# A two-block transformer with a product-key expert layer on one core: when weight halves are split, how a bias row is added, and when later weights are loaded

## What is computed

```python
for layer, mixer in ((0, nsa_mixer), (1, moba_mixer)):
    shift, scale, gate = split(silu(c) @ ada_w[layer] + ada_b[layer], 3)
    h = rms_norm(x, norm_g[layer]) * (1 + scale) + shift
    x = x + gate * mixer(h)                 # h @ w_in, attention, (o * silu(z)) @ w_out
shift1, scale1, gate1, shift2, scale2, gate2 = split(silu(c_2) @ w_ada + b_ada, 6)
h = rms_norm(x, norm1_g) * (1 + scale1) + shift1
x = x + gate1 * (concat(norm(o_a), norm(o_b)) @ w_out)   # windowed and 2-D neighbourhood attention
h2 = rms_norm(x, norm2_g) * (1 + scale2) + shift2
x = x + gate2 * peer(h2)                    # 16384 experts, 16 of them per head and token
out = rms_norm(x, final_g)
```

## Time and profile before

| what | value |
|---|---|
| median of 3 runs | 1426.58 us |
| the profiled execution | 1428.41 us, its span 1427.1 us |
| PE busy in the span | 1328.8 us (93%) |
| DVE busy | 1063.2 us (75%) |
| ACT busy | 588.9 us |
| POOL busy | 293.0 us |
| granted clock of PE over the span | 0.967 |

### The profile page before, as it was taken

One profiled execution on the slowest core, in us unless ns is written; L12 is line 12 of the kernel. 1 busy time (PEld: TensorE's weight loads), 2 busy tenths in 40 slices (PEclk: granted clock), 3 DMA queues, 4 the chain that ended last, 5 costly groups with the idle time before them and its releaser, 6 DMA issues.

```text
span 1427.1 us, 22339 instructions
## 1 busy us (share of the span) xinstructions
PE 1328.8 (93%) x8387; PEld 1136.2 (80%) x8387; DVE 1063.2 (75%) x2290; ACT 588.9 (41%) x1099; POOL 293.0 (21%) x205
## 2 busy tenths in 40 slices
PE   5899798988799789999999999999999999999997
PEld 5577665676378556999999999999998888888886
DVE  5687796676577666699977888888977676766676
ACT  0444483354413261545555444444443333333332
POOL 0443102340203003568993000000000000000000
PEclk9899899998899889999999999999999999999999
DMA  9767622575359712424544444444455555555552
GB/s 355 264 217 251 239 68 89 197 271 174 96 176 358 269 53 96 170 88 164 188 151 156 146 147 147 148 147 149 148 196 189 191 190 183 187 191 190 184 187 104
DMA packets 101185, 253.72 MB, mean 178 GB/s; under 512 B 9432, under 2 KB 16856, under 8 KB 100704
## 3 DMA queue, kind: packets, MB, share of 16 engines
q1 hardware_dynamic: 68672, 192.76, 39.6%
q10 hardware_dynamic: 32416, 59.66, 11.7%
HBM read 251.34 MB, written 1.05 MB: 177 GB/s over the span
## 4 chain that ended last, share of the span: by engine, by line
PE 71%; DVE 11%; issue 6%; DMA 5%; POOL 4%; ACT 3%; SPq 1%; POOLq 0%; DVEq 0%; ACTq 0%
PE bank L1679 25%; PE bank L1671 21%; PE bank L698 7%; PE bank L1950 4%; DMA arena<-in_w_ada 3%; PE bank L1112 3%; DVE arena L433 3%; DMA arena<-in_ada_w 2%; PE bank L724 2%; POOL u_lo L1711 2%; PE bank L933 1%; PE bank L806 1%; PE bank L1024 1%; POOL v_lo L1711 1%; DVE arena L975 1%
## 5 line engine op out<-in xcount | busy, mean ns | idle before, releaser
L1671 PE MATMUL bank<-h_hi,u_hi 128*128 128x256 f32 x632 | 182.8, 289 | 4.2 <-POOL u_lo L1711 2.9
L1671 PE MATMUL bank<-h_hi,u_lo 128*128 128x256 f32 x632 | 178.7, 283 | 0.0
L1671 PE MATMUL bank<-h_lo,u_hi 128*128 128x256 f32 x632 | 178.7, 283 | 0.0
L433 DVE SCALAR_TENSOR_TENSOR arena<-arena,silu_c 128x512 f32<-128x512 f32 x140 | 119.9, 856 | 29.4 <-DMA arena<-in_w_ada 15.1
L2133 POOL TENSOR_SCALAR stat<-stat 128x1 f32<-128x1 f32 x2 | 0.4, 190 | 657.0 <-ACT arena L2130 657.0
L1671 PEld LDWEIGHTS bank<-h_hi,u_hi 128*128 128x128 f32 x632 | 121.0, 191 | 5.0 <-issue 2.0
L1671 PEld LDWEIGHTS bank<-h_lo,u_hi 128*128 128x128 f32 x632 | 121.1, 192 | 0.0
L1671 PEld LDWEIGHTS bank<-h_hi,u_lo 128*128 128x128 f32 x632 | 120.9, 191 | 0.0
L1671 PE MATMUL bank<-h_hi,v_hi 128*128 128x256 f32 x392 | 112.9, 288 | 0.8 <-POOL v_lo L1711 0.8
L2046 ACT ACTIVATE u_hi<-raw 128x1024 fp32r<-128x1024 f32 x64 | 67.9, 1062 | 109.2 <-PE bank L1679 109.2
L2046 ACT ACTIVATE v_hi<-raw 128x1024 fp32r<-128x1024 f32 x64 | 67.9, 1062 | 106.0 <-PE bank L1679 106.0
(11 more groups left out here) (277 smaller groups left out, 3557.5 us busy)
## 6 DMA issues: line engine op xcount, KB each, us to landing
raw<-in_u SPq DMA_DIRECT2D x128, 512.0 KB, 3.5
raw<-in_v SPq DMA_DIRECT2D x128, 512.0 KB, 4.2
arena<-in_w_ada SPq DMA_DIRECT2D x96, 256.0 KB, 3.1
arena<-in_ada_w SPq DMA_DIRECT2D x64, 256.0 KB, 3.6
arena<-in_ada_w SPq DMA_DIRECT2D x12, 512.0 KB, 12.0
raw<-in_nsa_w_in ACTq DMA_DIRECT2D x3, 2048.0 KB, 9.4
arena<-in_moba_w_in ACTq DMA_DIRECT2D x3, 2048.0 KB, 12.7
arena<-in_w_in ACTq DMA_DIRECT2D x3, 2048.0 KB, 11.2
```

What stands on the lines that cost most here:

```text
L433: m = V.did(ve.scalar_tensor_tensor(out=acc, in0=src, scalar=factor, in1=acc, op0=ALU.mult, op1=ALU.add))
L1671: last = pe.matmul(zbank[k].t[:, 0:S], u[:, c, :], h[:, c, :], start=n == 0, stop=n == 3 * DC - 1)
```

## The change

- `project_split` calls `ahead.step()` after each quarter's last matmul of the second token half, instead of `ahead.step(4)` after all of them and after `run_later()`. `project_cols_split` steps before `run_later()` too.
- `normalised` (L615) uses `scalar_tensor_tensor` with the identity as both inputs instead of `tensor_scalar`.
- The bias matmul L452 goes. `gate_bias` is zero but for partition 0, where SP loads the bias row of the next gate piece; the first step of a gate piece is then chunk times scalar plus `gate_bias`, and the sum over partitions brings the bias in.
- Sums come due after 13.0 in place of 8.0, transposes after 10.5 in place of 8.5.
- Two tile loads of each mixer move from the z (or v) projections to the start of the attention.
- `trickle(1)` in place of `trickle(2)` in the first z projection; one `trickle(1)` more in each `gated_out`; `gated_out` begins with bank 0.

```diff
         for c in range(DC):
...
-            if c == 0:
+            if c:
+                V.need(m)
+                m = V.did(ve.scalar_tensor_tensor(out=acc, in0=src, scalar=factor, in1=acc, op0=ALU.mult, op1=ALU.add))
+            elif j % 6 < 4:
                 V.need(m_silu, acc_read[k])
                 m = V.did(ve.tensor_scalar(acc, src, factor, None, ALU.mult))
             else:
-                V.need(m)
-                m = V.did(ve.scalar_tensor_tensor(out=acc, in0=src, scalar=factor, in1=acc, op0=ALU.mult, op1=ALU.add))
+                V.need(m_silu, acc_read[k], bias_mark[0])
+                m = V.did(ve.scalar_tensor_tensor(out=acc, in0=src, scalar=factor, in1=gate_bias, op0=ALU.mult, op1=ALU.add))
+                load_bias(m)
...
-                T.need(b.free, m, m_ones, m_bias)
-                pe.matmul(b.t[:], ones[:], acc, start=True, stop=False)
-                acc_read[k] = bias_read[side] = T.did(pe.matmul(b.t[:], ones_row, bias_row, start=False, stop=True))
+                T.need(b.free, m, m_ones)
+                acc_read[k] = T.did(pe.matmul(b.t[:], ones[:], acc, start=True, stop=True))
...
-        acc_read[k] = soon(sum_partitions, 8.0)
+        acc_read[k] = soon(sum_partitions, 13.0)
...
+    def load_bias(free):
+
+        if gate_order:
+            layer, j = gate_order.pop(0)
+            src = a["ada_b"][layer:layer + 1] if layer < 2 else a["b_ada_2"]
+            Y.need(free)
+            bias_mark[0] = ld_bias.did(sy.dma_start(gate_bias[0:1, :], src[:, j * WT:(j + 1) * WT]))
...
-            m_diag[t] = V.did(ve.tensor_scalar(diagonal[t], ident[:], stat[:, t:t + 1], None, ALU.mult))
+            m_diag[t] = V.did(ve.scalar_tensor_tensor(out=diagonal[t], in0=ident[:], scalar=stat[:, t:t + 1], in1=ident[:],
+                                                      op0=ALU.mult, op1=ALU.mult))
...
                 if t == NT - 1 and c % 2 == 1:
                     split_read[s] = m = T.did(last)
+                    if ahead:
+                        ahead.step()
...
             run_later()
-            if ahead and t == NT - 1:
-                ahead.step(4)
...
-    TURN_LAG = 8.5
+    TURN_LAG = 10.5
...
         halves = [range(DC)] if rstd is None else [range(DC // 2), range(DC // 2, DC)]
+
+        turn["proj"] = 0
...
                 load_all(loads)
+                trickle(1)
...
-        project_cols_split(z0, z_cols(zT, 0), z1, (out0, out1))
-        project_cols_split(z1, z_cols(zT, 1), None, (moba_kv,))
+        project_cols_split(z0, z_cols(zT, 0), z1, (out0,), 1)
+        project_cols_split(z1, z_cols(zT, 1))
         run_later(True)
+        load_all((out1, moba_kv))
...
-        project_cols_split(moba_z0, z_cols(zT, 0), moba_z1, (moba_out1,))
-        project_cols_split(moba_z1, z_cols(zT, 1), None, (qa,))
+        project_cols_split(moba_z0, z_cols(zT, 0), moba_z1)
+        project_cols_split(moba_z1, z_cols(zT, 1))
         run_later(True)
+        load_all((moba_out1, qa))
...
-        project_cols_split(kb, kb_use, vb_tile, (mix_out1,))
+        project_cols_split(kb, kb_use, vb_tile)
...
-        project_split(vb_tile, v_use(vb), None, (query0,))
+        project_split(vb_tile, v_use(vb))
         m_vb = V.last()
         run_later(True)
+        load_all((mix_out1, query0))
```

More of the change, by code:

```diff
@@ L411, in ada_steps @@
         acc = ada_acc[k]
-        if j % 6 >= 4:
-            side = j % 2
-            settle(bias_read, side)
-            bsrc = a["ada_b"][layer:layer + 1] if layer < 2 else a["b_ada_2"]
-            Y.need(bias_read[side])
-            bias_row, ones_row = gate_bias[32 * side:32 * side + 1, :], ones[32 * side:32 * side + 1, :]
-            m_bias = ld_bias[side].did(sy.dma_start(bias_row, bsrc[:, j * WT:(j + 1) * WT]))
         for c in range(DC):
@@ L455, in sum_partitions @@
             ada_mark[layer, j] = b.free
-            pe_us[0] += 0.9 if j % 6 < 4 else 2.0
-        acc_read[k] = soon(sum_partitions, 8.0)
-        if j % 6 >= 4:
-            bias_read[j % 2] = acc_read[k]
+            pe_us[0] += 0.9
+        acc_read[k] = soon(sum_partitions, 13.0)
     def gate_of(layer, j):
@@ L466, in build @@
     gate_bias = carve([P, WT], layers)
-    ld_bias = [Load(nc, st, f"ld_bias{i}") for i in range(2)]
-    bias_read, gate_read = [None, None], [None, None]
+    ld_bias, bias_mark, gate_read = Load(nc, st, "ld_bias"), [None], [None, None]
+    gate_order = [(0, 4), (0, 5), (1, 4), (1, 5), (2, 4), (2, 5), (2, 10), (2, 11)]
+    def load_bias(free):
[4 more added lines that the diff above has]
+            bias_mark[0] = ld_bias.did(sy.dma_start(gate_bias[0:1, :], src[:, j * WT:(j + 1) * WT]))
     fillers = [(0, j) for j in range(6)] + [(1, j) for j in range(4)] + [(2, j) for j in range(4)] + [(1, 4), (1, 5)] + \
@@ L512, in first_sums @@
         m = T.did(last)
-        if which == 0:
-            bias_read[:] = [m, m]
-        else:
+        if which:
             acc_read[:] = [m, m]
@@ L772, in project_cols, with project_cols_split @@
                 load_all(loads)
-    def project_cols_split(tile, use, ahead=None, loads=()):
+    def project_cols_split(tile, use, ahead=None, loads=(), steps=2):
         if ahead and tile.n < 4:
@@ L785, in project_cols_split @@
             pe_us[0] += 2.9
-            run_later()
             if ahead:
                 ahead.step()
+            run_later()
             b.free = use(i, b.t[:, 0:S], m)
-            trickle(2)
+            trickle(steps)
             if i == 0:
@@ L1214, in build @@
         finish()
+        G.need(m_a)
+        m_zero = G.did(po.memset(gate_bias[:], 0.0))
         for tile in (kv0, q0, cmp0):
             tile.load(Y)
+        load_bias(m_zero)
         ask_chunks()
```

## The result

The changed kernel takes **1414.65 us** (median of 4 runs, 1413.32 to 1415.94) against 1426.23 for the kernel before (median of 4). The ratio is 0.9914, 95% interval 0.9896 to 0.9933, so it is 12.3 us faster, by the interval 10 to 15. I had said 1390 us and a range down from 1411: the direction was right, two thirds of the gain are missing, and the time lies outside the range. The profiled execution spans 1411.9 us, against 1427.1 in that of before.

A forecast was written before the change was run, and what follows sets the result against it. PE was the engine to watch in the first 568 us, with DVE making it late. The terms summed to 36.6 us off 1428.4, giving 1391.8, and 1.8 lower as a median: 1390 us, range 1374 to 1411.

The forecast's parts named there:

- Third mixer: Third mixer's projections: 4 MB of loads move out and PE's 4.1 us sum wait shrinks; 5.0 us won, between 0 and 6.
- rival A: DVE stays late on chunk waits, losing terms of first z projection, second mixer's start and third mixer; 1408 us, chance 0.22.
- Quarters split early: Projections: ACT's splits ahead of a copy shorten three PE waits for lo halves; 6.0 us won, plus 3.6 of clock.
- Bias matmul: Gate pieces: dropping the bias matmul saves PE 1.0 us at four of eight places; 4.0 us won.
- Transposes later: PE's wait for POOL before a transpose goes, as it now stands behind 8 more matmuls; 2.7 us won.
- Loads moved: Two loads issued as each attention begins share DMA engines with chunks; 1 us lost each, -3.0 in all.
- First mixer's z projection: Fewer filler steps and later loads bring the second compressed-score chain earlier; 6.5 us won, less 4.0 for DVE not following.
- End of the second attention: Only one gate sum is forced, so the output product starts near 373.5 instead of 380.73; 7.3 us, plus 1.5 of clock.
- The diagonal: Norms: the two-input form of L615 is blocked by POOL's split as well; 0 us won.
- rival B: The two-input diagonal escapes POOL's block and falls to about 0.3 us in three places; 1384 us, chance 0.10.
- Rival C: ACT's early splits wait for the tile's DMA, so 6.0 + 3.6 us are lost; 1400 us, chance 0.07.
- Rival D: Chunks starve behind moved loads as attentions begin, up to 20.7 us in each of three; 1452 us, chance 0.03.

The follow-up runs named there:

- e13: Kernel before with only the parts ordering DVE's filler work (three steps fewer, later sums, loads in attentions) and e1's two steps; ratio 0.986.
- e3: Changed kernel with the next tile's four quarters split together after the tile's last matmul, as before; ratio 0.9921.
- e6: e1 with the next tile's four quarters split together after the last matmul, as before; ratio 0.9828.
- e8: e1 with transposes as early as before (8.5 in place of 10.5); ratio 0.9816.
- e16: Kernel before with only five parts: early quarters, bias row, later transposes, bank 0, diagonal; ratio 0.9893.
- e7: e1 with the first mixer's two tile loads issued in its projections as before, the other four kept in the attentions; ratio 0.9774, 1397.34 us.
- e2: Changed kernel with all six moved tile loads issued where they were before; ratio 0.9897.
- e1: Changed kernel with three filler steps instead of one in the second mixer's output product, so 114 stand before the third mixer; ratio 0.9813, 1403.36 us.
- e4: Changed kernel with the gate pieces' bias added by a second matmul again; ratio 0.9919.
- e5: e1 with the three mixers' nine h_lo splits moved from POOL to DVE; ratio 0.9781, 1397.1 us.
- e9: e1 with the edits of both e5 and e7; ratio 0.9788.
- e15: e7 with only the three h_lo splits at the mixers' starts moved from POOL to DVE; ratio 0.9775.

## Why the prediction was wrong

The account, in us against before. The terms of the two halves were 19.3 (first z projection 6.5 - 4.0, second mixer 6.0, end of its attention 7.3 + 1.5, third mixer 5.0, loads -3.0) and 17.3 (6.0 + 3.6 + 4.0 + 2.7 + 1.0). Measured alone they are 20.0 and 15.3, each within its doubt of about 3. So 36.6 becomes 35.3; less 8.6 counted twice, 26.7; less 14.4 for the boundary at 112 (11.1 by the section in the traces), 12.3. The last two steps are differences of measured ratios, so the chain closes by construction; what it shows is that no third loss of their size is needed. That the halves come out so well is in part luck: by my terms e13's sections were to win 1.5, 13.8 and 4.0 us, and they won 4.1, 10.3 and 3.7. The first mixer's total is in part luck, too: the quarters, 3.2 us there, are 0.9 by e3 and nothing by e6, and the transposes, 2.7, are 3.9 by e8.

**The step that failed first is "Third mixer", 5.0 "between 0 and 6".** I followed the filler count to the second attention (87, 94, 96) and used it there; for the third mixer I priced only the bytes that moved out, and took the loss's end of the range as 0. The same count carried on gives 112 where there were 114, and a piece has 8 steps: a forced sum at the worst place, ahead of a burst. I did say of the second mixer that "a gate piece is complete with step 88"; the same sentence was due for 112. The range's slow end had to hold this case: 1390 + 5.0 + 10 = 1405, and with the 8.6 of the next point 1414.

**The second is the sum itself.** Each term was priced as if the others were not there, with -4.0 as the only deduction, in the first mixer. The halves cover each other by more, and in the second and third mixers too: second section -10.3 and -7.6 alone, -14.3 together; third -3.7 and -3.6 alone, -1.1 together. (The three sections make it 14.3 us, where the ratios say 8.6; e16's fast execution accounts for about 5 of that.) This is the mechanism of rival A (DVE stays late); I gave it 0.22 and tied it to chunk waits. DVE did wait for chunks 23.0 us (16.4 + 5.6 + 0.8 + 0.2) against my "under 12", nearly as long as the 22.5 of before. Putting the first mixer's loads back won 5.6 us (e7), putting all of them back nothing that can be measured (e2), and two steps in DVE's order 14 (e1), so I take the lateness to sit more in its order than in the chunks; the two were not separated further.

*Quarters split early* (6.0, clock 3.6). The mechanism was right in one place of three: the wait at 287.95 us, 2.89 us, is 0.91 now, and I had said 0.9. The other two are 1.24 and 1.98. For the last one DVE's splits stand behind a head norm that waits 1.53 us for POOL, so there ACT's early hi halves gain little. The fourth wait grew from 0.86 to 2.07, on the second quarter's lo half, which I had named as late next and not priced. In all PE's waits for u_lo fell by 3.3 us (9.5 to 6.2), not by 6.0. The clock over the 5 us behind the 0.91 wait is 1.00 instead of 0.76. Undone alone, all of it shows as 1 or 2 us in the time.

*Bias matmul* (4.0): 0.7 by e4, with some 4 us of doubt, so its size is open. *Transposes later* (2.7): 0.4 by e8; the first mixer gains 3.9, though PE waits 2.6 us for the copy L876 now, and the third gives it back. *Loads moved* (-3.0): they cost in the first attention, where PE's wait is 3.1 us longer than in e7; at the start of the second the wait is 4.1 us shorter than in e2.

*First mixer's z projection* (6.5): the second compressed-score chain begins at 153.92 us instead of 160.12, 6.2 us earlier where I had named about 10, and PE's wait on L1418 is gone.

*End of the second attention* (7.3 + 1.5). PE starts the output product at 355.44 us, behind the attention's last values, a wait of 2.90 us and one gate sum (a matmul is two records here, 2.08 us for both):

```profile
349.60 1.08 PE L933 MATMUL bank<-arena 128*64 128x256 f32 x8 [0.83 <-ACT arena L1027]
353.58 2.08 PE L447 MATMUL bank<-arena,ones 128*128 128x512 f32 x2 [2.90 <-DVE arena L422]
355.44 2.03 PE L1114 MATMUL bank<-arena 128*128 128x512 f32 x3
```

The wait was 5.57 and is 2.90, and the one matmul behind it takes 2.08 where sum and bias took 4.0. From the end of the last values to the output product it is 4.8 us, where I had said 3 at most and before it was 11.7. That makes 6.9 us for my 7.3, which by its own numbers (371.9 + 2.0) should have been 6.8. The attention's stretch is 8 us shorter than in the earlier trace rows, as forecast.

*The diagonal* (0) was right, and rival B did not come: L614 takes 2.42 us beside POOL's split. The row that I leaned on the earlier trace rows shows less than I took from it, since its two instructions start 0.01 us apart. The Trainium skill (SBUF — State Buffer, Who interferes with whom) says that a two-input DVE instruction contends with a GpSimd one that reads SBUF; by that rule the trace agrees, 2.42 against 0.35 us in e5. Rival C did not come (0.91). Rival D did, at a small part of its price: 3 us of wait as one attention begins, where it had up to 20.7 in each of three.

## What to carry to other kernels

Where filler work is doled out by a counter, count it to the end of the program and mark every place where a piece ends ahead of a burst: two steps more or less were worth 9 to 14 us here, more than any single part that was undone alone. Waits of one engine on another's order need not be independent: here 8.6 of 35.3 us were counted twice, so run the change's halves apart before adding their terms. And when an instruction on DVE takes seven times its usual time, look at what POOL runs beside it, and try moving that rather than changing the instruction's form; here it won 4.6 us on e1, and nothing on top of e7.

## What the runs showed of the hardware

The block between DVE and POOL didn't depend on the form of the small instruction. As a tensor_scalar with one SBUF tensor, L615 took 2.35 us beside POOL's split; as a two-input operation it takes 2.42, and 0.35 without POOL. The Trainium skill (SBUF — State Buffer, Who interferes with whom) says that a tensor_scalar, too, can enter a mode that uses the ports shared with GpSimd, when its operands meet that mode's conditions; by that rule both forms can be blocked, and the trace agrees with 2.35 and 2.42 us. The same split takes 2.35 us on POOL and 1.22 on DVE. With the 0.35 us of an unblocked L614 that is 1.57 us of DVE's time, less than the one blocked instruction took.

By its ratio the fastest kernel is the changed one with e1's and e7's edits, 1397.34 us: 0.9774 (0.9761 to 0.9787) of the kernel before, where the changed kernel has 0.9914. e5, e9 and e15 (0.9775 to 0.9788) can't be told from it. Open is why e5 and e7 don't add, and what keeps v_lo late in the third mixer (4.2 us as its last projection begins, 3.4 in its output product).
